# Seven-product pairs in five more feed-forward stages, with half-sized pieces of modulation weights

## The reference

```python
def swiglu(h, w_gu, w_down):
    gate, up = jnp.split(h @ w_gu, 2, axis=-1)
    return (jax.nn.silu(gate) * up) @ w_down
...
    for i in range(DEPTH):                     # DEPTH = 4
        x = x + 0.5 * swiglu(rmsnorm(x, ffn1_norm[i]), ffn1_w_gu[i], ffn1_w_down[i])
        ...                                    # mixer i: delta net, stick-breaking or sparse attention
        x = x + 0.5 * swiglu(rmsnorm(x, ffn2_norm[i]), ffn2_w_gu[i], ffn2_w_down[i])
```

```python
m = jnp.split((jax.nn.silu(c) @ mod_w[i] + mod_b[i])[:, None, :], N_MOD, axis=-1)
```

## Time and profile before

| | us |
|---|---|
| median of three runs | 3556.15 (3552.24 to 3557.05) |
| profiled execution, its own time | 3553.38 |
| its span | 3551.6 |
| PE busy | 3455.2 (97%) |
| DVE busy | 2462.3 (69%) |
| ACT busy | 1846.4 (52%) |
| POOL busy | 146.2 (4%) |
| DMA | 692.40 MB, mean 195 GB/s |

### The profile page before, as it was taken

The page is one execution under the profiler, slowest core; times in us unless marked ns, Lnnn a source line. Parts: engine busy times, 40 slices in busy tenths (PEclk is TensorE's granted clock), DMA queues, the critical chain, the costliest instruction groups (busy, mean ns, idle before and its releaser), DMA issues. The chain is left out here.

```text
span 3551.6 us, 45223 instructions
## 1 busy us (share of the span) xinstructions
PE 3455.2 (97%) x18348; PEld 2926.2 (82%) x18348; DVE 2462.3 (69%) x2743; ACT 1846.4 (52%) x2151; POOL 146.2 (4%) x152
## 2 busy tenths in 40 slices
PE   9999999999999999999999999999999999999999
PEld 7889888888888888888889878787888678788877
DVE  5776656666666678566677668787866567786586
ACT  5454444544645445545454456666664455655464
POOL 0001100000000000000001100000001000000000
PEclk9999999999999999999999999999999999999999
DMA  6642156664467763576752157575744147574574
GB/s 264 240 155 84 60 194 234 224 237 166 158 257 261 260 237 121 202 280 249 272 189 100 71 178 255 201 249 200 250 148 166 67 154 247 194 251 141 189 233 161
DMA packets 95741, 692.40 MB, mean 195 GB/s; under 512 B 10672, under 2 KB 10800, under 8 KB 12208
## 3 DMA queue, kind: packets, MB, share of 16 engines
q1 hardware_dynamic: 79344, 574.15, 43.0%
q0 software_dynamic: 16192, 115.35, 11.5%
HBM read 650.66 MB, written 1.05 MB: 183 GB/s over the span
## 5 line engine op out<-in xcount | busy, mean ns | idle before, releaser
L2391 DVE TENSOR_TENSOR w_lo<-raw,w_hi 128x2048 fp32r<-128x2048 f32 x468 | 1067.7, 2289 | 330.5 <-ACT w_hi L1662 330.3
L1662 ACT ACTIVATE w_hi<-raw 128x2048 fp32r<-128x2048 f32 (+1 forms) x470 | 895.4, 1909 | 372.0 <-PE acc L702 259.3
L700 PE MATMUL wrk<-w_hi,h_hi 128*128 128x512 f32 (+1 forms) x2040 | 795.4, 390 | 14.2 <-issue 5.4
L702 PE MATMUL wrk<-w_hi,h_lo 128*128 128x512 f32 (+1 forms) x2040 | 783.6, 384 | 0.0
L701 PE MATMUL wrk<-w_lo,h_hi 128*128 128x512 f32 (+1 forms) x2040 | 782.4, 384 | 0.0
L700 PEld LDWEIGHTS wrk<-w_hi,h_hi 128*128 128x128 f32 x2040 | 383.6, 188 | 95.1 <-issue 15.9
L700 PE MATMUL acc<-w_hi,hid_hi 128*128 128x512 f32 (+1 forms) x1160 | 454.4, 392 | 4.2 <-DVE hid_lo L2493 3.7
L702 PE MATMUL acc<-w_hi,hid_lo 128*128 128x512 f32 (+1 forms) x1160 | 450.9, 389 | 0.0
L701 PE MATMUL acc<-w_lo,hid_hi 128*128 128x512 f32 (+1 forms) x1160 | 450.6, 388 | 0.0
L702 PEld LDWEIGHTS wrk<-w_hi,h_lo 128*128 128x128 f32 x2040 | 383.3, 188 | 76.7
L701 PEld LDWEIGHTS wrk<-w_lo,h_hi 128*128 128x128 f32 x2040 | 383.9, 188 | 71.1 <-issue 0.2
(11 more groups left out here) (326 smaller groups left out, 4973.4 us busy)
## 6 DMA issues: line engine op xcount, KB each, us to landing
raw<-in_wts SPq DMA_DIRECT2D x469, 1024.0 KB, 4.9
arena<-in_mods POOLq DMA_DIRECT2D x72, 1024.0 KB, 5.1
arena<-in_wts SPq DMA_DIRECT2D x72, 1024.0 KB, 7.7
arena<-arena POOLq DMA_DIRECT2D x36, 1024.0 KB, 7.1
const<-in_const SPq DMA_DIRECT2D x1, 2112.0 KB, 17.4
c<-in_bias POOLq DMA_DIRECT2D x8, 256.0 KB, 3.0
x<-in_x SPq DMA_DIRECT2D x2, 512.0 KB, 6.9
c<-in_c SPq DMA_DIRECT2D x1, 1024.0 KB, 4.8
```

Source lines behind the costliest of these rows:

```text
L700: nc.tensor.matmul(o, l_h, r_h, start=first, stop=False, skip_group_check=True)
L702: return nc.tensor.matmul(o, l_l, r_h, start=False, stop=last, skip_group_check=True)
L1662: return nc.scalar.activation(o, i, f, **kw)
L2391: tt(w_lo[:, ns % SLOTS, :], v, w_hi[:, ns % SLOTS, :].bitcast(F32), ALU.subtract).then_inc(lo_ready, 1)
```

## The change

1. ffn1_1, ffn2_1, ffn1_2, ffn2_2 and ffn1_3 get pairs at steps 4 and 8, so their units are 0, 1, 2, 3, (4,5), 6, 7, (8,9), 10. They now run through `ffn_pairs`.
2. `m_raw` moves to `h_tok` and `m_prod` to `row`, outside the arena. There is room for two pieces of 512 KB, so that a piece is half of one before; most jobs write their product over the piece. A job is now one vector instruction, and from ffn2_1 on a piece has one job.
3. `mod_plan` deals a stage's jobs to the units by weights (0, 4, 6, 2, 0, 8, 2, 0, 6): 4, 6, 2, 8, 2, 6 of 28 jobs in ffn1_1, and 3, 6, 2, 7, 2, 6 of 26 in the four others. Half of a unit's jobs stand before the gating, half after the next piece's remainder.
4. GpSimd's two kinds of transfers are put in one order (`block_sum` and the loads), and the loads wait for the statistics of the stage instead of the tokens.
5. `factors_low` is cut in two halves, in all stages with pairs: the first at its old place, the second in the first pair behind `hid_low`. ScalarE's `part` waits for them.
6. ScalarE waits at the start of an FFN for the modulation jobs of the stages before.

```diff
@@ -57,7 +57,8 @@
...
-PAIRS = {n: (2, 5, 8) for n in ("ffn2_3", "b0_ctx", "b0_ffn0", "b0_ffn1", "b1_ffn0", "b1_ffn1")}
+PAIRS = {n: (4, 8) for n in ("ffn1_1", "ffn2_1", "ffn1_2", "ffn2_2", "ffn1_3")}
+PAIRS |= {n: (2, 5, 8) for n in ("ffn2_3", "b0_ctx", "b0_ffn0", "b0_ffn1", "b1_ffn0", "b1_ffn1")}
@@ -124,13 +125,22 @@
...
-MOD_JOBS = [(m, w) for m in range(MOD_PIECES) for w in range(2 if 2 * m < CTX_CHUNKS else 1)]
+MOD_JOBS = [(k, w) for k in range(2 * MOD_PIECES) for w in range(2 if k < CTX_CHUNKS else 1)]
...
     a = mod_start(name)
-    return [g for g, (m, _) in enumerate(MOD_JOBS) if a <= m < a + MOD_SHARE[name]]
+    return [g for g, (k, _) in enumerate(MOD_JOBS) if a <= k // 2 < a + MOD_SHARE[name]]
+def mod_plan(name):
+    plan, jobs = units(name), mod_jobs(name) if name in MOD_OPS else []
+    pair = [kind == "pair" for kind, _ in plan] + [False]
+    room = [0 if k == 0 or pair[k] else 2 if pair[k + 1] else 4 if k == 1 else 8 if pair[k - 1] and k + 1 < len(plan) else 6 for k in range(len(plan))]
+    ends = [len(jobs) * sum(room[:k + 1]) // sum(room) for k in range(len(plan))]
+    return [jobs[a:b] for a, b in zip([0] + ends, ends)]
 ARENA = 15104
@@ -471,7 +481,7 @@
         f_sq, f_rr = area(5120, 4 * T), area(6144, 4 * T)
-        m_raw, m_prod = area(3072, 2, PW), area(3072 + 2 * PW, 2, PW)
+        m_raw, m_prod = h_tok, row
         m_rows = c
@@ -935,7 +945,7 @@
                     pe.wait_ge(lo_ready, n + 1)
-                    pe.wait_ge(x_lo_ready, before(i, "paired") + 1)
+                    pe.wait_ge(x_lo_ready, 2 * before(i, "paired") + 1 + f // 2)
                     for q in range(4):
@@ -1854,6 +1864,7 @@
                     act.wait_ge(w_used, at(block, s) + 1)
+                    act.wait_ge(x_lo_ready, 2 * before(i, "paired") + 1 + (to is part_c))
                     fn(to, wrk[:, use[name, f"A{s}"] % BANKS, :], ACT.Copy).then_inc(part_out, 1)
@@ -2368,7 +2379,7 @@
             for i, (kind, name, prm) in enumerate(ops):
-                if kind in ("gdn", "sb", "dsa") and mods_before(i):
+                if kind in ("gdn", "sb", "dsa", "ffn") and mods_before(i):
                     act.wait_ge(mod_sums, mods_before(i))
@@ -2446,14 +2457,16 @@
...
-                m, w = MOD_JOBS[g]
-                l = 2 * m // (9 * KC)
-                dve.wait_ge(mod_landed[m % 2], 16 * (m // 2 + 1))
-                if g:
+                k, w = MOD_JOBS[g]
+                l = k // (9 * KC)
+                dve.wait_ge(mod_landed[k % 2], 16 * (k // 2 + 1))
+                v, last = m_raw[:, k % 2, :], g + 1 == len(MOD_JOBS) or MOD_JOBS[g + 1][0] != k
+                if not last and g > 1:
+                    dve.wait_ge(mod_sums, g - 1)
+                elif last and w:
                     dve.wait_ge(mod_sums, g)
-                for b in range(2):
-                    j = 2 * m + b - l * 9 * KC
-                    ins = stt(m_prod[:, b, 0:D], m_raw[:, m % 2, b * D:(b + 1) * D], 1.0, m_rows[:, w, :], ALU.mult, ALU.mult, accum_out=der[:, l, w, j:j + 1])
+                j = k - l * 9 * KC
+                ins = stt(v if last else m_prod[:], v, 1.0, m_rows[:, w, :], ALU.mult, ALU.mult, accum_out=der[:, l, w, j:j + 1])
                 ins.then_inc(mod_sums, 1)
@@ -2503,14 +2516,14 @@
                     hid_low(s - 1)
-                    for g in mine[:1]:
+                    for g in mine[:2]:
                         modulation(g)
...
                         split_to(ns + 3 * s + 3)
-                    for g in mine[1:]:
+                    for g in mine[2:]:
                         modulation(g)
@@ -2550,10 +2563,11 @@
...
-                def factors_low():
+                def factors_low(part):
+                    f = slice(2 * part, 2 * part + 2)
                     dve.wait_ge(x_hi_ready, before(i, "paired") + 1)
-                    tt(x_lo[:], x_sums, x_hi[:].bitcast(F32), ALU.subtract).then_inc(x_lo_ready, 1)
+                    tt(x_lo[:, f], x_sums[:, f], x_hi[:, f].bitcast(F32), ALU.subtract).then_inc(x_lo_ready, 1)
@@ -2598,10 +2612,12 @@
                         hid_low(q)
+                    if s == PAIRS[name][0]:
+                        factors_low(1)
                     split_to(n + 4)
                     dve.wait_ge(part_out, 3 * g + 1)
-                    dve.wait_ge(x_lo_ready, before(i, "paired") + 1)
+                    dve.wait_ge(x_lo_ready, 2 * before(i, "paired") + 2)
                     if s != PAIRS[name][0]:
@@ -2621,6 +2637,7 @@
                     dve.wait_ge(rstd_ready, 2 * before(i, "norm") + 2)
+                jobs = mod_plan(name)
                 factors()
@@ -2635,7 +2652,7 @@
                     if k == 1:
-                        factors_low()
+                        factors_low(0)
                     if name in AHEAD and s == AHEAD_AT:
@@ -2643,6 +2660,9 @@
                         add_blocks("T1", ahead)
+                    mine = jobs[k]
+                    for g in mine[:len(mine) // 2]:
+                        modulation(g)
                     if name == "b0_ctx" and s == FINAL_AT:
@@ -2652,6 +2672,8 @@
                     split_to(at("d", owed[-1]) + 1)
+                    for g in mine[len(mine) // 2:]:
+                        modulation(g)
                     if ahead is not None:
@@ -3388,25 +3410,42 @@
...
+            def block_sum(i, s, which):
+                g = starts[i]["pairs"] + PAIRS[ops[i][1]].index(s)
+                if which == "T3":
+                    pool.wait_ge(block_landed[HOME["B22"]], 16 * (g + 1))
+                    pool.wait_ge(sum_ready, 2 * g + 1)
+                else:
+                    pool.wait_ge(lo_ready, ring_at[i, ("B21", s)] + 1)
+                    pool.wait_ge(sum_ready, 2 * g + 2)
+                pool.dma_start(blocks[HOME[which]], blocks[HOME[ADDED[which]]], accum_op=ALU.add).then_inc(added[which], 16)
             def modulation(i, name):
-                start = mod_start(name)
                 if name in ROWS_IN:
                     pool.wait_ge(taken, use[name, "mrow3"] + 1)
-                if before(i, "x"):
-                    pool.wait_ge(x_new, before(i, "x"))
-                def load(m):
-                    pool.dma_start(m_raw[:, m % 2, :], mods_d[m]).then_inc(mod_landed[m % 2], 16)
-                end = start + MOD_SHARE[name]
-                load(start)
-                load(start + 1)
-                for g in mod_jobs(name):
-                    m, w = MOD_JOBS[g]
-                    if m + 2 < end and (g + 1 == len(MOD_JOBS) or MOD_JOBS[g + 1][0] != m):
-                        pool.wait_ge(mod_sums, g + 1)
-                        load(m + 2)
+                pool.wait_ge(rstd_ready, 2 * before(i, "norm") + 2)
+                end = 2 * (mod_start(name) + MOD_SHARE[name])
+                def load(k):
+                    v = mods_d[k // 2]
+                    pool.dma_start(m_raw[:, k % 2, :], v[:, k % 2 * D:(k % 2 + 1) * D]).then_inc(mod_landed[k % 2], 16)
+                load(2 * mod_start(name))
+                load(2 * mod_start(name) + 1)
+                plan = units(name) if name in PAIRS else []
+                jobs = mod_plan(name) if plan else [mod_jobs(name)]
+                for n, mine in enumerate(jobs):
+                    if n + 1 < len(plan) and plan[n + 1][0] == "pair":
+                        block_sum(i, plan[n + 1][1], "T3")
+                    if plan and plan[n][0] == "pair":
+                        block_sum(i, plan[n][1], "T4")
+                    for g in mine:
+                        k, w = MOD_JOBS[g]
+                        if k + 2 < end and (g + 1 == len(MOD_JOBS) or MOD_JOBS[g + 1][0] != k):
+                            pool.wait_ge(mod_sums, g + 1)
+                            load(k + 2)
@@ -3427,21 +3466,6 @@
                         load(n + 1)
-            def block_sums(i, name):
-                for k, s in enumerate(PAIRS[name]):
-                    g = starts[i]["pairs"] + k
-                    def add(which):
-                        pool.dma_start(blocks[HOME[which]], blocks[HOME[ADDED[which]]], accum_op=ALU.add).then_inc(added[which], 16)
-                    pool.wait_ge(block_landed[HOME["B22"]], 16 * (g + 1))
-                    pool.wait_ge(sum_ready, 2 * g + 1)
-                    add("T3")
-                    pool.wait_ge(lo_ready, ring_at[i, ("B21", s)] + 1)
-                    pool.wait_ge(sum_ready, 2 * g + 2)
-                    add("T4")
@@ -3454,8 +3478,10 @@
                     modulation(i, name)
-                if name in PAIRS:
-                    block_sums(i, name)
+                elif name in PAIRS:
+                    for s in PAIRS[name]:
+                        block_sum(i, s, "T3")
+                        block_sum(i, s, "T4")
```

## The result

The changed kernel takes 3719.02 us (median of 3 runs, 3714.34 to 3729.15) where the kernel before took 3556.15: 1.0473 of it, 95% interval 1.0458 to 1.0488. It is slower by 163 us, and I had forecast 67. The time lies above my range, which ended at 3650. The execution profiled took 3729.15 us.

The account below looks back on a forecast made before the run. TensorE bounds the kernel, busy 3455.2 of 3551.6 us. Stage costs 1.7 (ffn1_1) and 51 (four others) plus clock 15 made +68 us, forecast 3623; own bounds 3599 to 3649, with rival B 3570 to 3650.

Parts of the forecast that it names:

- saved by two pairs: Each of the five changed stages: 24 fewer products save 5.45 us, slower summed-factor products lose 0.6; 4.85 us saved.
- 1 start: Stage start: VectorE makes the factor sums ahead of the first gating, so TensorE waits; plus 0.9 us a stage.
- 2 first pair, T2: Pair at step 4: TensorE waits for T2's remainder, 2.1 us, plus one modulation job of 1.15; plus 3.3 us.
- 3 second pair, B21: Pair at step 8, after a unit owing one down piece: B21's remainder comes late; plus 2.3 us, 1.1 without the job.
- 4 unit 2: Unit 2, four stages from ffn2_1: third modulation jobs wait for landings, delaying remainders; 2.7 to 5.3 us, middle 4.0.
- 4 unit 6: Unit 6, same four stages: jobs waiting for landings delay the remainder TensorE needs; 0.9 to 3.4 us, middle 2.15.
- 4 unit 10: Last unit, same four stages: third job's landing delays hid_low; plus 6.3 us before a mixer, 3.6 before an FFN.
- clock, per stage: After some 18 TensorE pauses over 2 us, half clock loses 1.7 us each at one in two; 15 us in all.
- Step 4: Modulation in the four stages from ffn2_1: a group's third job waits for a 512 KB landing of 3.7 to 5.0 us.
- Rival B: Landings don't matter: VectorE meets no unlanded modulation piece; five stages at +1.7 and half of ten clock losses, 3573 us; chance 0.13.
- Rival C: Jobs move T2 and B21 into free time, pairs cost only the stage start; faster, 3536 us; chance 0.11.
- Rival D: Only the known 2.1 us pause returns; jobs and the single owed down piece cost nothing; 3551 us; chance 0.06.

Follow-up runs that it names:

- kernel with buffer and plan: Changed kernel with a third half-piece buffer and modulation jobs spread in smaller groups, VectorE and ScalarE in the change's order: 3557.37 us, 1.0010 of the kernel before.
- with buffer, plan and order mended: Changed kernel with third buffer, jobs spread, and VectorE and ScalarE work reordered at stage start and in pairs: 3526.93 us, 0.9928 of the kernel before.
- kernels with late and with split blocks: Changed kernel, one edit each: pairs' block loads issued about 16 us later, 3717.22 us; each block load split into two of 512 KB, 3699.71 us.

## Why the prediction was wrong

The direction, the places and the chain from a late landing over VectorE to TensorE were right. How long a landing takes beside other loads was not, nor what the clock adds, and the size is off by 96 us. Step by step, for ffn2_1 and ffn1_2 (pauses read from the starts of successive products in the trace, less the usual 0.23 us, with the slower first product behind a pause counted in):

| step | predicted | measured |
|---|---|---|
| saved by two pairs | 4.85 | 3.6 us less busy in the kernel with buffer and plan |
| 1 start | 0.9 | 1.2 |
| 2 first pair, T2 | 3.3 | 3.1, 3.2 |
| 3 second pair, B21 | 2.3 | 2.45 |
| 4 unit 2 | 4.0 (2.7 to 5.3) | 10.2 and 9.8 |
| 4 unit 6 | 2.15 (0.9 to 3.4) | 9.1 and 9.3 |
| 4 unit 10 | 3.6 before an FFN, 6.3 before a mixer | 6.9 and 9.4 |
| clock, per stage | 3 (15 in all, at most 31) | 11.3 and 13.2 |

- Steps 1 to 3 hold within 0.3 us. ffn1_1, which has two jobs to a piece and one landing wait of 1.1 us, was forecast at +1.7 without clock; its pauses are 8.2 us, less 4.85, and 2.5 us of clock (6.8 us at half of it): +5.9. Of these pauses 0.9 and 0.5 stand at places for which I had no step.
- ffn1_0, ffn2_0, ffn2_3 and the stages behind it: nothing, as forecast. So are 120 matmuls fewer and 144 loads.
- Step 4 is the one that failed: "the half piece shares the engines, at most with another 1.2 us: 5.0". That let a piece start moving beside block loads as early as alone, and gave each queue a half of the engines while its 512 KB pass. In the trace the first packet comes 3.6 to 3.9 us after the issue there instead of 1.2 to 1.4, which I had put at nothing; then the queue of modulation gets a third of the bytes and not a half; and when two pieces are in flight the second waits for the first. So 512 KB land in 8 to 12 us. Alone they take 3.8 to 4.0, and there my 3.7, read off between the rows of 256 and 1024 KB, was good. The rows had the hint: the earlier trace rows has 7.7 us for block loads against 4.9 for raw pieces, so the queue was already deep when blocks ran, and in the changed kernel the same row says 9.7.
- From that step the rest grows. Unit 2 was "just in time" at its first group with 3.7; with 8 us neither group is, and the second group's pieces are issued while the first's are still on their way, so it pays again. VectorE waits at eight to ten landings a stage where I had counted six. Unit 10 has no block loads, but the raw pieces of the next stage are under way there: its last piece starts 2.7 to 3.4 us after the issue and lands after 5.5 to 6.9, not 3.7, and that is most of the 3 us by which its row is off. In the table step 4 is 16 us a stage, some 65 us over four.
- The clock was the second mis-sized term. I priced every pause like the one of the earlier trace rows, 3.4 us of half clock at one in two. The pauses of 4.7 to 9.4 us bring 6.8 to 10.2 us of half clock each (one of 4.2 brought 3.4), 31 to 41 us a stage, and a stage's length less its pauses leaves 11 to 13 us for it. (TensorE stands still for part of that time: it is busy for 21.9 of the 30.7 us at half clock in ffn2_1 and for 29.2 of 41.0 in ffn1_2. That is why a third and not a half is lost.) Some 51 us in all against 15. The 65 and the 36 are 101; by medians I was off by 96, and the profiled execution is the longest of the three. (By its own terms the prediction's sum is 3624, not 3623.)
- The Trainium skill (TensorE: Matmul & The Clock Gate, The HAM clock gate) has the slow state as the default and activity as what lifts it; in the prediction it put the term nearer 31 than 15. This trace agrees in direction: the longer TensorE stood still, the longer the clock stayed at 0.50. It went past my upper end.
- The Trainium skill (DMA: Bandwidth & Descriptors, Queues, rings and completion order) says that a DMA engine takes turns between the queues it has work for, a packet at a time. Had I used it with the row lengths of the two queues, 4 and 8 KB, equal turns of one row each would have given modulation a third of the bytes, not a half. The runs agree while both queues move: 109 packets each and 0.45 of 1.26 MB with rows of 8 KB in the blocks, 171 and 173 packets and half of the bytes with rows of 4 KB. By my own estimate that share alone would have made the 5.0 a 6.2 (512 KB at a third of 425 GB/s take 1.2 us longer than at a half); the rest of the 8 us is the late first packet.
- Rival B is out (144 us hang on the landings). Its sum, 3573, is close to what the kernel with all jobs and no landing to wait for took, 3574.6. Rival C is out for the change as it was made, since in its order neither B21 nor T2 is in time; with buffer, plan and order mended the kernel is faster by 0.7%. Rival D is out too; only the pairs without jobs are near no change, 1.0007.

The 18 us that the jobs cost without landings can be read from the two traces. The five stages differ by 22.7 us: TensorE stands idle for 11.6 us more, and is busy for 11.0 more, with 30.6 us at half clock against 6.8. They belong to where the jobs stood, since the kernel with buffer and plan has all the jobs and is at 1.0010.

What stays open: why the first packet starts 2.5 us later beside block loads than alone. Nor was it tried what raw pieces in rows of 4 KB would give on top of the blocks, or to issue the modulation loads ahead of the blocks.

## What to carry to other kernels

Price a small load beside large ones by what it takes while the others are full, not by a time read when the queue was alone: when its first packet starts, its share by packets (short rows get fewer bytes), and how many of its own pieces are ahead of it. A share read over a window can hide a stretch in which the queue moves nothing; cut the window at the first packet. An in-order engine that both feeds TensorE and consumes late transfers should never stand at such a transfer with a needed remainder behind it: three buffers, with the jobs spread in groups no larger than that, were worth 162 of 163 us here. Look at the order on that engine before adding more of a thing that saves products: moving a few instructions gave 0.5% in the kernel before, where ten more pairs by themselves gave nothing.

## What the hardware showed that I had not expected

- Two queues, both moving: equal turns by packet, 109 and 109 with rows of 4 KB against 8 KB (0.45 of 1.26 MB), 171 and 173 with 4 KB against 4 KB (0.63 of 1.25 MB).
- The first packet of a load issued by POOL to its empty queue started 1.2 to 1.4 us after the issue where the weights' queue moved at most 74 packets in that time (35 loads), 2.4 to 3.4 us after it where it moved 103 to 138 (20 loads), and 3.6 to 3.9 us after it beside block loads, where it moved 173 to 196 (9 loads). 512 KB landed in 3.8 to 4.0 us alone and in 8 to 12 us beside block loads.
- Pieces issued 0.8 to 1.0 us behind one of POOL's own transfers for T3 landed after 9.4 to 10.9 us, with that transfer (8.4 to 10.6 us) ahead of them in the queue. It cost nothing here, since no job needed them so soon.
- A longer pause of TensorE costs more clock as well: 3.4 us at 0.50 after 2.1 us, 6.8 to 10.2 around pauses of 4.7 to 9.4. In ffn1_1 6.8 us at half clock cost about 3: the stage took 192.7 with them, and 189.7 and 189.1 in the kernels with late and with split blocks, which had the same waits there and none of the low clock.
